# Another search for the selection threshold: six counts placed by secants instead of eight by halving

## The chip, the cores and the metric

The kernel runs on one core of a Trainium2 chip. The metric is the device time of one execution in microseconds (us); the value quoted is the median of several executions of the same program on the same core.

## What is computed

The reference is two transformer-like blocks of a sequence of 2048 rows of width 1024, one after the other. Only the attention of the second block matters here. For each query row it scores all earlier keys with an indexer of eight small heads, keeps the 256 keys with the highest scores, and attends to these alone:

```python
TOPK_MAX = 256
...
logits = jnp.einsum('bqhd,bsd->bqhs', qib.astype(jnp.float32), kf_idx) * (IDX_DIM ** -0.5)
score = jnp.einsum('bqhs,bqh->bqs', jax.nn.relu(logits),
                   wb.astype(jnp.float32)) * (N_IDX_HEADS ** -0.5)
causal = key_pos[None, :] <= q_pos[:, None]
score = jnp.where(causal[None], score, -jnp.inf)
_, sel = lax.top_k(score, k_top)
...
s = jnp.einsum('bqhgd,bqkhd->bqhgk', qg, k_sel.astype(jnp.float32)) * (HEAD_DIM ** -0.5)
s = jnp.where(valid[:, :, None, None, :], s, -jnp.inf)
p = jax.nn.softmax(s, axis=-1)
o = jnp.einsum('bqhgk,bqkhd->bqhgd', p, v_sel.astype(jnp.float32))
```

Here `k_top` is 256, and `k_sel`, `v_sel` are the keys and values picked by `sel`.

## The kernel before

The program is a chain of phases: a convolution mixer, projections, a first attention, projections and rotation of the second block, then `phase_select_attend` (L2359 to L3197), which is the phase of this change, and `phase_out_2`, the last projection. In the trace `phase_select_attend` runs from about 2300 us to 3013 us.

It works on 16 blocks of 128 queries. They are taken in the order `ORDER` (L1927): 0, 1, 4, 6, 8, 10, 12, 14, 15, 13, 11, 9, 7, 5, 3, 2. Block b (its place in that order) has `keys(b)` = 128 × (ORDER[b] + 1) keys, so that the blocks grow from 128 keys to 2048 (b = 8) and shrink again to 384 (b = 15). Keys come in groups of 512 (`GROUP`): blocks 0, 1, 14 and 15 have one group, 2, 3, 12 and 13 two, 4, 5, 10 and 11 three, 6 to 9 four. A block is worked off in four pairs of heads, and a pair in as many steps as it has groups. All engines run through the same written-out list of steps (`units`), each with its own instructions and with semaphores between them. `in_quarter(u, pair, quarter)` picks the step in which a piece of side work is done: quarter q of a pair with G groups is the step q·G//4. With four groups the four quarters are four steps; with three groups quarters 0 and 1 are the same step; with two groups 0 and 1 are one and 2 and 3 the other; with one group all four are one step.

In a step the PE makes score products into five PSUM buffers (L3152, L3153): attention products of a block 1.6 pairs ahead, and indexer products of a block three blocks ahead. VectorE masks the attention products and keeps the row extreme (`mask`, L2918), ScalarE takes the exponential (`raise_e`, L2766), the PE transposes it (L3174), ScalarE copies it out (L2783), and the PE multiplies it with the values (L3188). ScalarE rectifies the indexer products (L2775) and VectorE adds them, weighted, to the score rows of 128 × keys(b) (`add_score`, L2896 and L2899).

14 blocks (2 to 15) have more than 256 keys and need a selection. While block b is attended to, the selection of block b + 1 (`now`) is finished and the threshold of block b + 2 (`soon`) is searched.

The search of `soon` before the change:

- ScalarE sums a sample of the scores (L2796) and the squares (L2803). The Pool makes the mean, a first guess from the normal distribution, and eight halving step widths from the deviation (`start_search`, L2678 to L2690).
- Eight counts follow, each a pass over the whole score row of 128 × keys: four on ScalarE (`count_signs`, L2823: the sum of the signs of guess minus score), in pair 1, quarters 0 and 2, and pair 2, quarters 0 and 2; four on VectorE (`count_at`, L2935: the number of scores at or above the guess), in pair 3, quarters 0 to 3.
- After each count but the last the guess goes up or down by one width. For a count of ScalarE the step is made in two instructions by ScalarE itself (L2827, L2829) in the five blocks 2, 3, 4, 5 and 15 (`local`), and by the Pool (`move_on`, L2697, L2698) in the nine blocks 6 to 14 (`pooled`). For a count of VectorE it is made in two instructions by VectorE (L2938, L2940).

Then the Pool turns the eight counts into missing keys (`sum_up`, L2664 to L2666), and VectorE takes the lowest guess with fewer than 256 keys at or above it, the edge, and the number of keys missing there (`find_edge`, L2948, L2952). Up to 16 missing keys are found by two rounds of the eight largest scores below the edge (L2969, L2977). `set_bias` (L2984, VectorE, pair 1, quarter 3) writes the mask of the block, `keep_causal` (L2727, Pool) its causal part, and the semaphore `biased` lets VectorE go on in `check_selection` (pair 2, quarter 1, at the start of the step), which also reads one number from the Pool (`find_rank`). If some row of the block has no guess with 1 to 16 missing keys, `check_selection` runs `search` and `break_ties` (L2986 to L3028) on VectorE: 31 rounds of a count and three small instructions, one after another. 

The Pool's program is one list: for each block `sum_up` and `rank_wanted` of `now`, `find_mean` and `start_search` of `soon`, `find_rank` of `now`, then the moves of `soon`, with `keep_causal(now)` ahead of the third move (k == 2).

Of the kernel before, what the change touches and what calls it, by code (L numbers as in the profile page):

```python
# [9 lines left out]
ALU = mybir.AluOpType  # L10
# [2348 lines left out]
def phase_select_attend(nc, sem, p_t, rot_hi, rot_lo, bit_int, bit_val, half_powers, rank_row, inverse_t, mix_t, ident, space, w_out):  # L2359
# [14 lines left out]
    COUNTS = 8  # L2374
    ON_ACT = COUNTS // 2
    OVER = 2.0 * SEQ
    EIGHT = 8
    SAMPLE = 4
# [125 lines left out]
    with ExitStack() as ctx:  # L2504
# [30 lines left out]
        halves = al.sb("sa_halves", [P, COUNTS])  # L2535
        width = al.sb("sa_width", [P, 2, COUNTS])
        guess = al.sb("sa_guess", [P, 2, COUNTS])
        go_d = al.sb("sa_go_d", [P, 1])
        go_a = al.sb("sa_go_a", [P, 1])
        go_p = al.sb("sa_go_p", [P, 1])  # L2540
        signs = al.sb("sa_signs", [P, 2, ON_ACT])
        count = al.sb("sa_count", [P, 2, COUNTS - ON_ACT])
        even = al.sb("sa_even", [P, TILES])
# [24 lines left out]
        counted, moved, signed, turned_up = sem("sa_counted"), sem("sa_moved"), sem("sa_signed"), sem("sa_turned_up")  # L2568
# [69 lines left out]
        def _(pool):  # L2638
# [8 lines left out]
            for qb in selecting:  # L2647
                nc.gpsimd.memset(even[:, qb:qb + 1], float(keys(qb) - 2 * TOP) + 0.5).then_inc(consts_set, 1)
# [6 lines left out]
            pool.wait_ge(bits_in, 64)  # L2655
# [22 lines left out]
            def start_search(b):  # L2678
# [8 lines left out]
                then(nc.gpsimd.tensor_scalar(width[:, j], halves[:], sd[:, 0:1], (4.0 if keys(b) < 2 * TOP - P // 2 else 1.25) * SMALL, ALU.mult, ALU.mult))  # L2687
# [760 lines left out]
```

## Time and profile before

| what | us |
|---|---|
| median of 3 runs | 3189.06 |
| lowest and highest run | 3187.68, 3195.86 |
| span of the profiled execution | 3189.0 |
| of it PE busy | 2990.2 (94%) |
| VectorE (DVE) busy | 2253.7 (71%) |
| ScalarE (ACT) busy | 1624.1 (51%) |
| Pool busy | 231.3 (7%) |

The page gives the profiled execution its span, from the first instruction to the last, and no second time; it lies 0.06 us under the median of the runs. "Busy" is the time in which an engine executes instructions; waits for semaphores are not in it. The shares are means over phases of different kinds, so the rows further down are those of the selection phase.

### The profile page before, as it was taken

The page shows a single profiled execution, that of the slowest core. Times are in us where ns is not written, and L with a number is a line of the kernel's source. Part 1 is how long each engine was busy: PE and PEld are TensorE (multiplying, and loading weights), DVE is VectorE, ACT ScalarE, POOL GpSimd, SP SyncE. Part 2 cuts the span into 40 slices and gives each one's busy share as a digit, 9 for nine tenths or more (in the row PEclk, how much of TensorE's full clock was granted, in tenths as well). Part 3 has the DMA queues.
Part 4 walks back from the last instruction along what each step waited for, and adds up shares of the span by engine and source line. Part 5 has one row for each costly group of instructions (what it writes and reads, how often), then busy time and mean ns, then how long its engine had stood idle before and what let it go on. Part 6 is the DMA issues. An engine that isn't in the chain of part 4 may idle for free. (4 is left out here: it accounts for less than half of the span.)

```text
span 3189.0 us, 48176 instructions
## 1 busy us (share of the span) xinstructions
PE 2990.2 (94%) x17460; PEld 2369.3 (74%) x17460; DVE 2253.7 (71%) x3296; ACT 1624.1 (51%) x2947; POOL 231.3 (7%) x519
## 2 busy tenths in 40 slices
PE   6999999999998999999999999999977889998899
PEld 5888788888777866677777777887756666776687
DVE  8888877753677758888878554524378989988543
ACT  5344422232545436777769423211288887887500
POOL 0000000000000001110100000000021321213100
PEclk8999999999999999999999999999989999999899
DMA  4434422244657432111136334232641111011665
GB/s 119 121 109 122 145 67 75 84 141 144 170 171 254 154 131 77 32 37 41 45 92 199 112 96 132 86 132 74 172 98 34 31 28 24 23 36 39 170 183 158
DMA packets 377860, 331.47 MB, mean 104 GB/s; under 512 B 100988, under 2 KB 331900, under 8 KB 371472
## 3 DMA queue, kind: packets, MB, share of 16 engines
q1 hardware_dynamic: 371784, 293.40, 32.4%
q0 software_dynamic: 5120, 34.67, 2.8%
q8 instruction: 142, 2.33, 0.3%
q14 instruction: 94, 0.77, 0.1%
q10 hardware_dynamic: 720, 0.31, 0.1%
HBM read 211.26 MB, written 107.10 MB: 100 GB/s over the span
## 5 line engine op out<-in xcount | busy, mean ns | idle before, releaser
L629 PE MATMUL p_oa_acc<-s_h_a_hi,s_mx_w_hi 128*128 128x512 f32 x768 | 301.8, 393 | 15.2 <-DVE s_h_a_lo L418 9.4
L323 ACT ACTIVATE s_mx_w_hi<-s_mx_raw 128x512 fp32r<-128x512 f32 x224 | 139.1, 629 | 320.6 <-PE p_oa_acc L629 256.8
L629 PE MATMUL p_oa_acc<-s_h_a_lo,s_mx_w_hi 128*128 128x512 f32 x768 | 300.4, 391 | 0.0
L629 PE MATMUL p_oa_acc<-s_h_a_hi,s_mx_w_lo 128*128 128x512 f32 x768 | 300.2, 391 | 0.0
L1598 DVE TENSOR_TENSOR_SCAN s_st_prod<-s_st_soft,s_st_prod 128x512 f32<-128x512 f32 x192 | 234.4, 1267 | 15.9 <-ACT s_st_soft L1525 15.9
L3174 PE MATMUL p_sa_turn<-s_ident,s_sa_arg 128*128 128x128 f32 x1088 | 166.3, 289 | 48.5 <-ACT s_sa_prob L2783 30.9
L1525 ACT ACTIVATE s_st_soft<-p_st_z 128x512 f32<-128x512 f32 (+3 forms) x320 | 153.7, 534 | 112.0 <-PE p_st_z L1650 112.0
L2345 PE MATMUL p_pr_ps<-s_h_hi,s_pr_w_hi 128*128 128x512 f32 (+1 forms) x712 | 195.4, 395 | 1.8 <-PEq L1712 1.2
L2766 ACT ACTIVATE s_sa_arg<-s_sa_arg,s_sa_low_top 128x128 f32<-128x128 f32 (+15 forms) x128 | 155.7, 1218 | 79.6 <-DVE s_sa_low_top L2918 79.6
L460 DVE TENSOR_TENSOR s_mx_w_lo<-s_mx_raw,s_mx_w_hi 128x512 fp32r<-128x512 f32 x224 | 153.5, 685 | 57.8 <-ACT s_mx_w_hi L323 56.3
L2345 PE MATMUL p_pr_ps<-s_h_lo,s_pr_w_hi 128*128 128x512 f32 (+1 forms) x712 | 191.5, 389 | 0.0
L2345 PE MATMUL p_pr_ps<-s_h_hi,s_pr_w_lo 128*128 128x512 f32 (+1 forms) x712 | 191.5, 389 | 0.0
L3174 PEld LDWEIGHTS p_sa_turn<-s_ident,s_sa_arg 128*128 128x128 f32 x1088 | 120.9, 145 | 86.4 <-issue 53.3
L2227 DVE TENSOR_TENSOR s_pr_w_lo<-s_pr_raw,s_pr_w_hi 128x1024 fp32r<-128x1024 f32 (+1 forms) x22 | 26.5, 1204 | 223.5 <-ACT s_pr_w_hi L2168 223.5
L629 PEld LDWEIGHTS p_oa_acc<-s_h_a_hi,s_mx_w_hi 128*128 128x128 f32 x768 | 145.0, 189 | 47.9 <-issue 17.9
L2775 ACT ACTIVATE s_sa_relu<-p_sa_pr 128x512 f32<-128x512 f32 (+3 forms) x304 | 155.5, 567 | 28.0 <-DVE s_sa_score L2899 13.8
L629 PEld LDWEIGHTS p_oa_acc<-s_h_a_hi,s_mx_w_lo 128*128 128x128 f32 x768 | 145.1, 189 | 30.4
L3188 PE MATMUL p_sa_o_sum<-s_sa_prob,s_sa_v_nat 128*64 128x128 f32 x2176 | 160.7, 288 | 7.4 <-ACT s_sa_o L2789 7.4
L629 PEld LDWEIGHTS p_oa_acc<-s_h_a_lo,s_mx_w_hi 128*128 128x128 f32 x768 | 145.2, 189 | 29.6
L2899 DVE SCALAR_TENSOR_TENSOR s_sa_score<-s_sa_relu,s_sa_w_idx,s_sa_score 128x1024 f32<-128x1024 f32 (+7 forms) x154 | 153.8, 1021 | 18.9 <-ACT s_sa_relu L2775 17.9
L3188 PEld LDWEIGHTS p_sa_o_sum<-s_sa_prob,s_sa_v_nat 128*64 128x64 f32 x2176 | 121.2, 141 | 58.9 <-issue 46.3
L2783 ACT ACTIVATE s_sa_prob<-p_sa_turn 128x512 f32<-128x512 f32 (+3 forms) x320 | 154.3, 541 | 11.2 <-PE p_sa_turn L3174 10.7
(379 smaller groups left out, 7408.7 us busy)
## 6 DMA issues: line engine op xcount, KB each, us to landing
s_mx_raw<-in_w_in_a SPq DMA_DIRECT2D x128, 256.0 KB, 3.8
s_pb_ada<-in_w_ada SPq DMA_DIRECT2D x16, 768.0 KB, 4.3
s_pr_raw<-in_w_in SPq DMA_DIRECT2D x21, 512.0 KB, 3.9
s_pr_work<-s_pr_stage SPq DMA_DIRECT2D x38, 256.0 KB, 4.2
d_rot_hi<-s_pr_rot POOLq DMA_DIRECT2D x9, 1024.0 KB, 4.3
d_rot_lo<-s_pr_stage POOLq DMA_DIRECT2D x9, 1024.0 KB, 6.2
d_y_t<-s_mx_y SPq DMA_DIRECT2D x16, 512.0 KB, 5.5
s_oa_y_raw<-d_y_t SPq DMA_DIRECT2D x16, 512.0 KB, 4.8
```

What stands on the lines that cost most here:

```text
L323: nc.scalar.activation(w_hi[:, m], raw[g % 2][:, m], ACT.Copy).then_inc(hi_done, 1)
L460: nc.vector.tensor_tensor(w_lo[:, m], raw[g % 2][:, m], w_hi[:, m].bitcast(F32), ALU.subtract).then_inc(lo_done, 1)
L629: ins = nc.tensor.matmul(bank, w[:, m, k, :], a[:, m, k, :], start=(k == 0 and n == 0), stop=(k == KH - 1 and n == 2))
L1525: nc.scalar.activation(soft[:, u % DEEP, s, 0:n], z[u % 2 * 2 + s][:, 0:n], ACT.Sigmoid, scale=-SCALE).then_inc(softened, 1)
L1598: nc.vector.tensor_tensor_scan(prod[:, b, s, 0:n][:, ::-1], back, back, carry, ALU.mult, ALU.bypass).then_inc(multiplied, 1)
L2345: ins = nc.tensor.matmul(ps[b % 2][0:cols, t * 512:(t + 1) * 512], w[b % 2][:, k, 0:cols], a[:, k, t * 512:(t + 1) * 512], start=(k == 0 a ...
L2766: nc.scalar.activation(row, row, ACT.Exp, scale=-1.0, bias=low_top[:, s % DEEP, side, len(parts(qb)) - 1:len(parts(qb))], accum_out=total[ ...
L2775: nc.scalar.activation(relu[:, a % R_DEEP, half:half + n], pr[p % BANKS][:, 0:n], ACT.Relu).then_inc(relu_done, 1)
L2783: nc.scalar.activation(prob[:, u % P_DEEP, side, 0:w], turn[turn_of["prob", u, side] % 2][:, 0:w], ACT.Copy).then_inc(p_ready, 1)
L2899: ins = nc.vector.scalar_tensor_tensor(s, relu[:, a % R_DEEP, 0:n], w, s, ALU.mult, ALU.add)
L3174: ins = nc.tensor.transpose(turn[i % 2][:, c:c + P], arg[:, s % DEEP, side, at + c:at + c + P], ident[:])
L3188: ins = nc.tensor.matmul(o_ps[side * HD:side * HD + HD, pair * P:pair * P + P], v_nat[:, (at + c) // P, kv * HD:kv * HD + HD], prob[:, u % ...
```

## The change

The number of counts goes from eight to six: three on ScalarE (pair 1, quarters 0 and 2; pair 2, quarter 0) and three on VectorE (pair 2, quarter 2; pair 3, quarters 0 and 2). All five moves between them are made by the Pool, in all 14 blocks, and their size comes from the number of keys missed: the first by the slope of the normal distribution, the next two by a secant through the last two counts, with its slope held between a quarter and four times the normal one, the last two by the last slope, damped by 0.7 and 0.5. The aim is 248 keys (256 − 8). A secant needs one over the square of the rise; VectorE makes it (`flatten`, one RECIPROCAL of 128 × 1) between two instructions of the Pool, in pair 1, quarter 3, and pair 2, quarter 1. The Pool's `keep_causal(now)` stays ahead of the third move, and so behind the first secant. `find_edge` waits for all five moves instead of for VectorE's own steps. The constants for the halving (one small DMA, 14 memsets) go away.

```diff
-    COUNTS = 8
-    ON_ACT = COUNTS // 2
+    COUNTS = 6
+    ON_ACT = 3
+    STEEP, FLAT = 0.25, 4.0
+    SECANTS, DAMPED = 2, {3: 0.7, 4: 0.5}
-    pooled = [b for b in selecting if b - 2 in blocks and keys(b - 2) >= WIDE]
-    local = [b for b in selecting if b not in pooled]
+    MOVES = COUNTS - 1
+    def aim(qb):
+        return float(keys(qb) - 2 * (TOP - EIGHT))
+    def first_slope(qb):
+        at = start_point(qb)
+        return math.sqrt(2.0 * math.pi) * math.exp(at * at / 2.0) / (2.0 * (keys(qb) - P // 2))
...
-                then(nc.gpsimd.tensor_scalar(width[:, j], halves[:], sd[:, 0:1], (4.0 if keys(b) < 2 * TOP - P // 2 else 1.25) * SMALL, ALU.mult, ALU.mult))
+                for n, share in enumerate((1.0, STEEP, FLAT)):
+                    then(nc.gpsimd.tensor_scalar(slopes[:, j, n:n + 1], sd[:], first_slope(b) * share * SMALL, None, ALU.mult))
...
             def move_on(b, k):
-                at, step, half = guess[:, j, k:k + 1], width[:, j, k:k + 1], width[:, j, k + 1:k + 2]
-                pool.wait_ge(signed, ON_ACT * i + k + 1)
-                then(nc.gpsimd.tensor_scalar(go_p[:], signs[:, j, k:k + 1], float(keys(b) - 2 * TOP) + 0.5, step, ALU.is_lt, ALU.mult))
-                nc.gpsimd.tensor_scalar(guess[:, j, k + 1:k + 2], go_p[:], half, at, ALU.subtract, ALU.add).then_inc(moved_on, 1)
+                at, here, to = guess[:, j, k:k + 1], level[:, j, k:k + 1], guess[:, j, k + 1:k + 2]
+                if k < ON_ACT:
+                    pool.wait_ge(signed, ON_ACT * i + k + 1)
+                    then(nc.gpsimd.tensor_scalar(here, signs[:, j, k:k + 1], -aim(b), None, ALU.add))
+                else:
+                    pool.wait_ge(counted, (COUNTS - ON_ACT) * i + k - ON_ACT + 1)
+                    then(nc.gpsimd.tensor_scalar(here, count[:, j, k - ON_ACT:k - ON_ACT + 1], -2.0, keys(b) - aim(b), ALU.mult, ALU.add))
+                if k == 0:
+                    then(nc.gpsimd.tensor_scalar(move[:], here, slopes[:, j, 0:1], None, ALU.mult))
+                elif k <= SECANTS:
+                    then(nc.gpsimd.tensor_scalar(rise[:], here, level[:, j, k - 1:k], None, ALU.subtract))
+                    nc.gpsimd.tensor_scalar(square_rise[:], rise[:], rise[:, 0:1], 1.0, ALU.mult, ALU.max).then_inc(risen, 1)
+                    then(nc.gpsimd.tensor_scalar(run[:], at, guess[:, j, k - 1:k], rise[:, 0:1], ALU.subtract, ALU.mult))
+                    pool.wait_ge(flattened, SECANTS * i + k)
+                    then(nc.gpsimd.tensor_scalar(slope[:], run[:], per_rise[:, 0:1], slopes[:, j, 1:2], ALU.mult, ALU.max))
+                    then(nc.gpsimd.tensor_scalar(slope[:], slope[:], slopes[:, j, 2:3], None, ALU.min))
+                    then(nc.gpsimd.tensor_scalar(move[:], here, slope[:, 0:1], None, ALU.mult))
+                else:
+                    then(nc.gpsimd.tensor_scalar(move[:], here, slope[:, 0:1], DAMPED[k], ALU.mult, ALU.mult))
+                nc.gpsimd.tensor_scalar(to, move[:], -1.0, at, ALU.mult, ALU.add).then_inc(moved_on, 1)
...
-                for k in range(ON_ACT):
+                for k in range(MOVES):
                     if k == 2 and now in selecting:
                         keep_causal(now)
-                    if soon in pooled:
+                    if soon in selecting:
                         move_on(soon, k)
...
             def count_signs(b, k):
-                if k and b in pooled:
-                    act.wait_ge(moved_on, ON_ACT * pooled_to(b) + k)
-                elif k:
-                    act.wait_ge(turned_up, done)
+                if k:
+                    act.wait_ge(moved_on, MOVES * i + k)
...
-                if b in pooled:
-                    return
-                act.wait_ge(signed, ON_ACT * i + k + 1)
-                nc.scalar.activation(go_a[:], c, ACT.Sign, scale=-1.0, bias=even[:, b:b + 1]).then_inc(turned_up, 1)
-                act.wait_ge(turned_up, done + 1)
-                nc.scalar.activation(guess[:, j, k + 1:k + 2], go_a[:], ACT.Identity, scale=width[:, j, k + 1:k + 2], bias=at).then_inc(turned_up, 1)
...
-                for k, (pair, quarter) in enumerate(((1, 0), (1, 2), (2, 0), (2, 2))):
+                for k, (pair, quarter) in enumerate(((1, 0), (1, 2), (2, 0))):
                     if in_quarter(u, pair, quarter) and soon:
                         count_signs(soon, k)
...
+            def flatten(b, k):
+                dve.wait_ge(risen, SECANTS * place_of(b) + k)
+                nc.vector.reciprocal(per_rise[:], square_rise[:]).then_inc(flattened, 1)
+
             def count_at(b, k):
+                dve.wait_ge(moved_on, MOVES * i + k)
...
-                if k + 1 < COUNTS:
-                    dve.wait_ge(counted, steps * i + c + 1)
-                    nc.vector.tensor_scalar(go_d[:], total_k, float(TOP), width[:, j, k:k + 1], ALU.is_ge, ALU.mult).then_inc(moved, 1)
-                    dve.wait_ge(moved, done + 1)
-                    nc.vector.tensor_scalar(guess[:, j, k + 1:k + 2], go_d[:], width[:, j, k + 1:k + 2], at, ALU.subtract, ALU.add).then_inc(moved, 1)
...
                 if in_quarter(u, 1, 3) and now:
                     set_bias(now)
-                for k, (pair, quarter) in enumerate(((3, 0), (3, 1), (3, 2), (3, 3))):
+                for k, (pair, quarter) in enumerate(((1, 3), (2, 1))):
+                    if in_quarter(u, pair, quarter) and soon:
+                        flatten(soon, 1 + k)
+                for k, (pair, quarter) in enumerate(((2, 2), (3, 0), (3, 2))):
                     if in_quarter(u, pair, quarter) and soon:
                         count_at(soon, ON_ACT + k)
```

## Rows read from the trace of the kernel before

**Rows 1.** The page's first line.
```profile
span 3189.0 us, 48176 instructions
```

**Rows 2.** Stretches, one per block (1, 4, 6, 8), and the sum of all 16.
```profile
2345.00:2379.00 34.00, 23.61 (x121) 18.00 (x122) 27.20 (x66) 26.72 (x69) 9.94 (x23) 0.85 0.28 55
...
2472.00:2528.00 56.00, 47.58 (x336) 36.22 (x334) 51.84 (x95) 46.84 (x91) 15.37 (x31) 0.97 0.14 29
...
2586.00:2651.00 65.00, 55.64 (x436) 41.62 (x435) 60.20 (x112) 52.97 (x95) 14.07 (x30) 1.00 0.12 26
...
2713.00:2773.00 60.00, 57.41 (x500) 45.18 (x499) 54.76 (x111) 51.38 (x89) 13.20 (x31) 1.00 0.12 28
...
sum 690.00, PE 594.59 PEld 460.05 DVE 585.06 ACT 559.53 POOL 163.38; mean PE 37.16 PEld 28.75 DVE 36.57 ACT 34.97 POOL 10.21
```

The columns of rows 2 are: stretch, its length, then busy us (and instructions) of PE, PE weight load, DVE, ACT, POOL, then TensorE's granted clock, the DMA share and GB/s.

**Rows 3.** Waits of DVE, then of PE, 2310 to 3010 us: total, times, longest.
```profile
DVE s_sa_arg L2918 <- PE p_sa_pr L3153: 49.7, 57, 3.6
DVE s_sa_score L2899 <- ACT s_sa_relu L2775: 16.5, 12, 2.4
...
PE p_sa_pr L3152 <- DVE s_sa_low_top L2918: 30.9, 24, 4.2
```

**Rows 4.** Groups by line on DVE, 2310 to 3010 us: busy, mean ns, idle before.
```profile
L2935 DVE TENSOR_SCALAR_CACHE_REDUCE s_sa_junk_d<-s_sa_score,s_sa_guess 128x640 bf16<-128x640 f32 (+13 forms) x56 | 82.7, 1477 | 0.8
...
L2940 DVE TENSOR_SCALAR s_sa_guess<-s_sa_go_d,s_sa_width,s_sa_guess 128x1 f32<-128x1 f32 x42 | 11.5, 273 | 1.5
...
L2938 DVE TENSOR_SCALAR s_sa_go_d<-s_sa_count,s_sa_width 128x1 f32<-128x1 f32 x42 | 9.0, 214 | 1.5
...
L2935 DVE DVE_READ_ACCUMULATOR s_sa_junk_d<-s_sa_score,s_sa_guess 128x1 f32 x56 | 4.7, 83 | 0.0
L3045 DVE RECIPROCAL s_sa_inverse<-s_sa_total 128x8 f32<-128x8 f32 x16 | 3.2, 198 | 1.2 <-ACT s_sa_arg L2766 1.2
```

**Rows 5.** Groups by line on ACT, 2310 to 3010 us.
```profile
L2823 ACT ACTIVATE s_sa_junk_a<-s_sa_score,s_sa_guess 128x640 bf16<-128x640 f32 (+13 forms) x56 | 74.2, 1324 | 0.3 <-POOL s_sa_guess L2698 0.2
...
L2823 ACT ACTIVATION_READ_ACCUMULATOR s_sa_junk_a<-s_sa_score,s_sa_guess 128x1 f32 x56 | 12.0, 214 | 0.0
...
L2829 ACT ACTIVATE s_sa_guess<-s_sa_go_a,s_sa_guess,s_sa_width 128x1 f32<-128x1 f32 x20 | 7.7, 387 | 0.7
L2827 ACT ACTIVATE s_sa_go_a<-s_sa_signs,s_sa_even 128x1 f32<-128x1 f32 x20 | 5.9, 295 | 0.6
```

**Rows 6.** Groups by line on POOL, 2310 to 3010 us.
```profile
L2698 POOL TENSOR_SCALAR s_sa_guess<-s_sa_go_p,s_sa_width,s_sa_guess 128x1 f32<-128x1 f32 x36 | 14.2, 393 | 3.8
L2697 POOL TENSOR_SCALAR s_sa_go_p<-s_sa_signs,s_sa_width 128x1 f32<-128x1 f32 x36 | 14.0, 388 | 132.6 <-ACT s_sa_junk_a L2823 132.6
```

**Rows 7.** Instructions of L2727: shortest, median and longest in ns, first and last start.
```profile
L2727 POOL TENSOR_SCALAR_AFFINE_SELECT s_sa_bias<-s_sa_bias x14: 294/1196/1199, 2355.2 to 2973.8; 128x128 bf16<-128x128 bf16 x14
```

**Rows 8.** In order of time, block 2 (two groups): start us, length us.
```profile
2394.12 0.63 DVE L2984 TENSOR_SCALAR s_sa_bias<-s_sa_place 128x896 bf16<-128x896 f32 x1
...
2395.39 0.19 ACT L2823 ACTIVATION_READ_ACCUMULATOR s_sa_junk_a<-s_sa_score,s_sa_guess 128x1 f32 x1
...
2398.28 0.08 DVE L2918 DVE_READ_ACCUMULATOR2_ANT s_sa_low_top<- 128x1 f32 x1
...
2400.48 0.22 ACT L2823 ACTIVATION_READ_ACCUMULATOR s_sa_junk_a<-s_sa_score,s_sa_guess 128x1 f32 x1
```

**Rows 9.** The same of block 4 (three groups); in brackets idle time before and releaser.
```profile
2499.81 0.19 ACT L2823 ACTIVATION_READ_ACCUMULATOR s_sa_junk_a<-s_sa_score,s_sa_guess 128x1 f32 x1
...
2501.37 1.15 DVE L2899 SCALAR_TENSOR_TENSOR s_sa_score<-s_sa_relu,s_sa_w_idx,s_sa_score 128x896 f32<-128x896 f32 x1 [1.72 <-ACT s_sa_relu L2775]
```

**Rows 10.** The same of block 6 (four groups).
```profile
2614.66 0.22 ACT L2823 ACTIVATION_READ_ACCUMULATOR s_sa_junk_a<-s_sa_score,s_sa_guess 128x1 f32 x1
...
2616.39 1.16 DVE L2984 TENSOR_SCALAR s_sa_bias<-s_sa_place 128x1920 bf16<-128x1920 f32 x1
```

More of the change, by code:

```diff
@@ L2534, in phase_select_attend @@
         sd = al.sb("sa_sd", [P, 1])
-        halves = al.sb("sa_halves", [P, COUNTS])
-        width = al.sb("sa_width", [P, 2, COUNTS])
+        slopes = al.sb("sa_slopes", [P, 2, 3])
         guess = al.sb("sa_guess", [P, 2, COUNTS])
-        go_d = al.sb("sa_go_d", [P, 1])
-        go_a = al.sb("sa_go_a", [P, 1])
-        go_p = al.sb("sa_go_p", [P, 1])
+        level = al.sb("sa_level", [P, 2, COUNTS])
+        rise = al.sb("sa_rise", [P, 1])
+        square_rise = al.sb("sa_square_rise", [P, 1])
+        per_rise = al.sb("sa_per_rise", [P, 1])
+        run = al.sb("sa_run", [P, 1])
+        slope = al.sb("sa_slope", [P, 1])
+        move = al.sb("sa_move", [P, 1])
         signs = al.sb("sa_signs", [P, 2, ON_ACT])
         count = al.sb("sa_count", [P, 2, COUNTS - ON_ACT])
-        even = al.sb("sa_even", [P, TILES])
         lack = al.sb("sa_lack", [P, COUNTS])
@@ L2646, in _ @@
             nc.gpsimd.memset(tiny_var[:], 1e-12).then_inc(consts_set, 1)
-            for qb in selecting:
-                nc.gpsimd.memset(even[:, qb:qb + 1], float(keys(qb) - 2 * TOP) + 0.5).then_inc(consts_set, 1)
             for qb in blocks:
@@ L2841, in _ @@
             act.dma_start(v_raw[:, 0], p_t[ROW_V:ROW_V + P, 0:GROUP]).then_inc(v_in[0], 16)
-            for to, rows in ((halves, half_powers), (ranks, rank_row), (bit_i, bit_int), (bit_f, bit_val)):
+            for to, rows in ((ranks, rank_row), (bit_i, bit_int), (bit_f, bit_val)):
                 act.dma_start(to[:], rows.partition_broadcast(P)).then_inc(bits_in, 16)
@@ L2911, in mask @@
                     else:
-                        dve.wait_ge(consts_set, 2 + len(selecting) + qb)
+                        dve.wait_ge(consts_set, 2 + qb)
                 dve.wait_ge(product, p + 1)
@@ L2919, in mask @@
                                                scalar=before, op0=ALU.add, op1=ALU.min, accum_out=low_top[:, s % DEEP, side, m:m + 1]).then_inc(masked, 1)
+            def flatten(b, k):
+                dve.wait_ge(risen, SECANTS * place_of(b) + k)
+                nc.vector.reciprocal(per_rise[:], square_rise[:]).then_inc(flattened, 1)
             def count_at(b, k):
                 n, i, j, c = keys(b), place_of(b), b % 2, k - ON_ACT
[L2924 to L2932 removed]
+                dve.wait_ge(moved_on, MOVES * i + k)
                 if c == 0 and i >= 2:
                     dve.wait_ge(lacking, i - 1)
[L2935 to L2940 removed]
+                nc.vector.tensor_scalar(junk_d[:, 0:n], score[:, b % AHEAD, 0:n], guess[:, j, k:k + 1], None, ALU.is_ge, ALU.add,
+                                        accum_out=count[:, j, c:c + 1]).then_inc(counted, 1)
             def find_edge(b):
@@ L2944, in find_edge @@
                 dve.wait_ge(lacking, i + 1)
-                dve.wait_ge(moved, 2 * (COUNTS - ON_ACT - 1) * (i + 1))
+                dve.wait_ge(moved_on, MOVES * (i + 1))
                 if i:
@@ L3413, in program @@
             space.before_selection(Alloc(nc, third))
-            phase_select_attend(nc, between, p_t, rot_hi, rot_lo, a["bit_int"], a["bit_val"], a["half_powers"], a["rank_row"], inverse_t, mix_t, ident,
+            phase_select_attend(nc, between, p_t, rot_hi, rot_lo, a["bit_int"], a["bit_val"], a["rank_row"], inverse_t, mix_t, ident,
                                 space, a["w_out_2"][0])
```

28 lines of the change are left out of this document (7 added, 21 removed).

## The prediction

> **What bounds the kernel now.** The sum goes by the profiled execution, whose span [rows 1] is the median of the runs to 0.1 us. I read first the busy time of the stretches between blocks, because the change touches one phase of about 700 us. Over its 16 blocks no engine is full: of 690 us PE is busy 595, DVE 585, ACT 560, the Pool 163 [rows 2]. It differs by block. In block 1 none reaches 81%; in blocks 4 and 6 DVE leads with 93%, PE has 85%; in block 8 PE leads with 96%, DVE has 91% [rows 2]. So DVE or ACT time taken away is worth most in the small blocks and the rise, and little in the middle. Next the waits: DVE stands 49.7 us waiting for score products and 16.5 us for rectified scores, and PE stands 30.9 us because DVE has not emptied a product buffer [rows 3]. DVE and PE wait for each other in turns, so a DVE delay can be made up only partly, and a DVE saving is passed on only partly. Then the groups by line give the prices, and the order of time gives the places where the new waits fall.
>
> **What goes.** On DVE, one count in four: (82.7 + 4.7)/4 = 21.9 us; 42 steps, 11.5 + 9.0 = 20.5 us; and the gaps ahead of these, about 3 us [rows 4]. That is 45.4 us. On ACT, one count in four, (74.2 + 12.0)/4 = 21.6 us, and the 20 own steps, 7.7 + 5.9 = 13.6 us: 35 us [rows 5]. The removed DMA and memsets lie ahead of the first block, while the engines wait for other loads: nothing.
>
> **What comes.** DVE gets 28 reciprocals of 128x1. The nearest row is one of 128x8 at 198 ns [rows 4]: 5.5 us at most, and I take that. DVE is 40 us lighter. Spread over blocks (the count by its keys, the rest evenly, 1.3 us each): 13.7 us in the four-group blocks 6 to 9, 12.0 in the three-group ones (4, 5, 10, 11), 14.1 in the six of one or two groups (0 to 3, 12, 13).
>
> The Pool gets 25 instructions of one column a block for its moves (3 + 8 + 8 + 3 + 3) and two more slopes: 14 × 27 = 378 for 72. One costs 0.39 us and a gap of 3.8/36 = 0.11: 0.5 us [rows 6]. That is some 150 us more, and 163 + 150 still is under half of 690: the Pool does not become the bound by its sum. Its replies matter.
>
> **New waits.** A secant is a round trip: ACT counts, the Pool makes three instructions (1.5 us), DVE the reciprocal, the Pool four more (2.0 us). DVE waits in its fixed order, and behind it wait the adds and masks that empty the product buffers, so PE too.
>
> (a) First reciprocal, behind `set_bias`. In block 2 ACT's second count is read out at 2395.6; plus 1.5 is 2397.1. DVE ends `set_bias` at 2394.75 [rows 8]: it stands 2.3 us. This is the pattern of the five blocks with one or two groups that have both selections (1, 2, 3, 12, 13), where count and reciprocal fall in one step or nearly: 11.5 us. In block 6 the count ends at 2614.9, the square is there at 2616.4, and `set_bias` runs until 2617.55 [rows 10]: nothing, and so in the blocks of three and four groups.
>
> (b) Second reciprocal. In block 2 it comes behind a mask that ends at 2398.4, and ACT's third count ends at 2400.7, so the square at 2402.2 [rows 8]: 3.8 us. The later two-group blocks have shorter counts; I take 2.5 for each of the four. Blocks 0 and 1, where the next count also sits in the same step and needs the four last Pool instructions: 2 us each. Together 14 us. With three groups, the square in block 4 would be there at 2501.5, and DVE already stood idle until 2501.37, for ACT [rows 9]: nothing. With four groups the count is a step ahead: nothing.
>
> (c) `biased`. `keep_causal` is now behind the first secant. After the reciprocal it is 2.0 us of moves and up to 1.2 us of its own [rows 7], 3.2 us; DVE has two adds or so before `check_selection` (about 1.9 us). In the nine blocks with fewer than four groups the check is in the very next step: 1.3 us each, 11.7 us. With four groups a step lies between.
>
> Together 37 us of DVE standing, as against 40 us of DVE work. That is why this is no simple gain.
>
> **The sum.** Savings: in the four-group blocks PE is as full as DVE, so half, 6.9 us; with three groups two thirds, 8.0; in the small blocks all, 14.1; 29 us. ACT's 35 us: 16.5 us of DVE's idle time are for ACT's relu [rows 3], part of it behind a count, as in block 4 [rows 9]; one of four counts goes: 3 us. Together 32 us. Waits: DVE stands now for PE 49.7 us in 57 places [rows 3], and a stand of 2 us just ahead of one of these is free; I let a third of the 37 us vanish so: 25 us stay. Net 7 us: **3189 − 7 = 3182 us**. A measurement of this kernel can tell about 0.3%, 9.6 us, from no change, so the likeliest reading is "within". The bounds: all of 40 us and no wait, 3149; half of the DVE saving and all waits, 3206.
>
> **Where row and rule meet.** The same `keep_causal` of 128x128 takes 294 ns at its shortest and 1196 ns in the median [rows 7], so a Pool instruction can be stretched fourfold by what runs beside it. The mean of 0.39 us for a one-column step holds such stretches at the rate they had. The Trainium skill (GPSIMD Engine Reference, Specifications) says that the Pool shares its SBUF interfaces with VectorE and is in contention with DVE instructions that have two SBUF inputs. The rows agree. That rule speaks against moving steps to the Pool; what it gives is the third rival. It holds least where it would hurt most: while DVE stands in (a) or (b) it runs nothing that could be in the way.
>
> **Rivals.**
> 1. *The waits are hidden* (0.22). The stands fall where DVE would have waited for PE; for: 49.7 us of such idle time. Savings of three quarters, 30 us, plus 3 of ACT, minus 6: 3162 us.
> 2. *The waits stay, the other side* (0.17). A stand of DVE in pair 1, quarter 3, or pair 2, quarter 1, fills the five product buffers, PE stops, and ACT's exponentials come later, so that the next count comes later as well. For: PE already stands 30.9 us for a mask [rows 3]. Savings at half, 20 us, waits whole, 37: 3206 us. It decides from the point where DVE stands longer than PE needs to fill the five buffers.
> 3. *The Pool is stretched* (0.04). Each of its chain's seven instructions takes 1.2 instead of 0.5 us: (a) and (b) 2.1 us longer at 11 places, (c) 2.8 at nine: 48 us, two thirds on the path: 3214 us.
> 4. *The search misses* (0.05). One row without a guess that misses 1 to 16 keys sets off 31 rounds on DVE, each a mean count of 1.56 us and three small steps of 0.25 [rows 4]: 72 us a block. 3182 + 72 = 3254 us. Against it: with 384 keys, of which the first row of the block sees 257, and normal scores, the guesses find by my working 199, 230 and 242 keys, inside the window of 240 to 255 at the third of six counts; bigger blocks start closer. But eight halvings cannot run away, and secants on a skewed row can.
>
> **Chances.** The forecast holds 0.52: 0.13 of it below 3179.5, 0.38 within 9.6 us of no change, 0.01 above. Rival 1 is faster (0.22); rival 2 slower by 0.15 and within by 0.02; rivals 3 and 4 slower (0.09). So faster 0.35, within 0.40, slower 0.25. The range goes from 3165, short of rival 1, to 3206, rival 2: below it lies 0.10, above it rivals 3 and 4. The forecast's own range is 3173 to 3192.
>
> **What would show it.** DVE busy in the phase falls by 40 us, ACT by 35, the Pool rises by 150. The waits list shows the reciprocal on DVE waiting for the Pool, some 25 us in 11 to 14 places, all in blocks of one or two groups, and DVE waiting for `biased` after it. Blocks 6 to 9 get shorter by about 1.7 us each, blocks 1 to 3, 12 and 13 stay or grow. I am wrong if the reciprocal's waits are under 10 us or over 45, if blocks of four groups show them, if the Pool's mean is above 0.6 us, or if rows of `search` appear.

## The result and the profile after

| | before | after |
|---|---|---|
| median of the runs, us | 3189.06 (3187.68 to 3195.86, 5 runs) | 3204.92 (3197.91 to 3208.25, 5 runs) |
| span of the profiled execution, us | 3189.0 | 3202.9 |

The ratio is 1.0041, with a 95% interval of 1.0027 to 1.0056: the changed kernel is 0.4% slower, 13 us (the two medians lie 16 us apart). The time lies inside the range, at its upper end, and on the other side of no change than the forecast. It is almost the time of rival 2 (3206 us).

The page of the changed kernel, its first line and its part 1:

```profile
span 3202.9 us, 48344 instructions
...
PE 3004.3 (94%) x17460; PEld 2384.2 (74%) x17460; DVE 2215.4 (69%) x3212; ACT 1596.7 (50%) x2879; POOL 335.6 (10%) x811
```

DVE is busy 38 us less than before, ACT 27 less, the Pool 104 more. PE is busy 14 us more. The selection phase grew from 713 us (2300 to 3013) to 727:

```profile
2300.00:3027.00 727.00, 623.50 (x4610) 487.44 (x4611) 558.22 (x1168) 548.55 (x1079) 270.81 (x697) 0.91 0.23 51
```

So the work went as intended and the time did not. The same blocks as in [rows 2], 1, 4, 6 and 8, same columns, in the changed kernel:

```profile
2348.00:2388.00 40.00, 27.02 (x122) 20.75 (x121) 24.76 (x60) 23.26 (x59) 18.22 (x50) 0.70 0.25 49
2485.00:2543.00 58.00, 50.15 (x336) 38.39 (x334) 47.93 (x89) 45.59 (x88) 22.63 (x50) 0.91 0.13 29
2602.00:2662.00 60.00, 55.09 (x441) 41.99 (x439) 56.91 (x113) 51.44 (x94) 22.41 (x51) 1.00 0.12 28
2721.00:2778.00 57.00, 56.29 (x498) 44.97 (x496) 52.02 (x111) 49.61 (x86) 18.04 (x51) 1.00 0.13 30
```

Block 1 takes 6 us more and block 4 two, blocks 6 and 8 take 5 and 3 less. I took the length of each block from the starts of ACT's copies of the outputs (15 starts in each trace), and that of block 0 from PE's first instruction of the phase, which starts at 2300.4 us before and in the changed kernel, and at 2304.3 us in the profiled execution of `six_halving`. By the number of groups, in us against before:

| blocks | changed kernel | `six_halving`, below |
|---|---|---|
| four groups (6 to 9) | −13.9 | −14.9 |
| three groups (4, 5, 10, 11) | +4.1 | −7.5 |
| one or two groups (0 to 3, 12 to 14) | +24.0 | −9.0 |

What takes the time back stands in the list of waits of the changed kernel, 2310 to 3030 us (total, times, longest):

```profile
ACT s_sa_arg L2788 <- DVE s_sa_low_top L2931: 92.8, 63, 7.1
...
DVE s_sa_per_rise L2937 <- POOL s_sa_square_rise L2712: 54.7, 19, 7.6
...
DVE s_sa_arg L2931 <- PE p_sa_pr L3162: 42.0, 54, 3.0
...
PE p_sa_pr L3161 <- DVE s_sa_low_top L2931: 36.3, 22, 5.2
...
DVE s_sa_arg L2931 <- issue: 20.0, 8, 3.4
...
DVE s_sa_junk_d L2945 <- POOL s_sa_guess L2720: 9.3, 11, 1.8
```

Against [rows 3]: the wait for products fell from 49.7 to 42.0 us and PE's wait for a mask rose from 30.9 to 36.3. New are 54.7 us ahead of the reciprocals and 9.3 us ahead of DVE's counts for a guess of the Pool. "issue" in front of a mask is the stand ahead of `check_selection`, which waits for `biased` and reads a number before it; it was 4.9 us in 5 places before. DVE's wait for ACT's relu, 16.5 us before, is 1.5 us.

The "issue" row holds only a part of the stands for `biased`. In block 4 the same stand is named after a product:

```profile
2510.95 0.29 POOL L2749 TENSOR_SCALAR_AFFINE_SELECT s_sa_bias<-s_sa_bias 128x128 bf16<-128x128 bf16 x1
...
2512.28 0.75 DVE L2931 CUSTOM_DVE_ANT_0 s_sa_arg<-p_sa_pr,s_sa_bias,s_sa_low_top 128x512 f32<-128x512 f32 x1 [2.60 <-PE p_sa_pr L3162]
```

The mask comes 1.04 us after the end of `keep_causal`. Read in order of time, a mask starts 1.03 to 1.71 us after that end, with idle time of over 0.15 us before it, in all 14 blocks that have a selection to finish, under either name. I call this idle time the mask stand. It sums to 31.3 us in the changed kernel and to 10.8 us (9 blocks) in the kernel before.

The moved work in order of time, block 2 (start, length; in brackets idle time before and who ended it):

```profile
2404.71 0.19 ACT L2842 ACTIVATION_READ_ACCUMULATOR s_sa_junk_a<-s_sa_score,s_sa_guess 128x1 f32 x1
...
2405.01 0.39 PE L3161 MATMUL p_sa_pr<-s_sa_ki_qi_q 128*128 128x512 f32 x1
...
2405.68 0.30 POOL L2712 TENSOR_SCALAR s_sa_square_rise<-s_sa_rise 128x1 f32<-128x1 f32 x1
...
2406.02 0.16 DVE L2937 RECIPROCAL s_sa_per_rise<-s_sa_square_rise 128x1 f32<-128x1 f32 x1 [2.29 <-POOL s_sa_square_rise L2712]
2406.10 1.82 DVE L2912 SCALAR_TENSOR_TENSOR s_sa_score<-s_sa_relu,s_sa_w_idx,s_sa_score 128x1024 f32<-128x1024 f32 x2
...
2406.44 1.56 POOL L2715 TENSOR_SCALAR s_sa_slope<-s_sa_run,s_sa_per_rise,s_sa_slopes 128x1 f32<-128x1 f32 x1
...
2408.10 0.29 POOL L2716 TENSOR_SCALAR s_sa_slope<-s_sa_slope,s_sa_slopes 128x1 f32<-128x1 f32 x1
...
2409.09 0.29 POOL L2749 TENSOR_SCALAR_AFFINE_SELECT s_sa_bias<-s_sa_bias 128x128 bf16<-128x128 bf16 x1
2410.77 0.69 DVE L2931 CUSTOM_DVE_ANT_0 s_sa_arg<-p_sa_pr,s_sa_bias 128x512 f32<-128x512 f32 x1 [2.85 <-issue]
...
2411.61 0.77 PE L3161 MATMUL p_sa_pr<-s_sa_k_hi,s_sa_ki_qi_q 128*128 128x512 f32 x1 [4.20 <-DVE s_sa_low_top L2931]
```

These 7 us show the first reciprocal and the mask stand. ACT's count ends at 2404.90. Three Pool instructions later DVE, which stood 2.29 us, makes the reciprocal and two adds; the Pool makes four more instructions of its chain and `keep_causal`, which ends at 2409.38. The first mask of the next step comes only at 2410.77. Then PE, which stood 4.20 us with its buffers full, takes 0.77 us for a product that took 0.39 us before the stand.

Block 4 has three groups, and its second reciprocal:

```profile
2513.46 0.09 DVE L2931 DVE_READ_ACCUMULATOR2_ANT s_sa_low_top<- 128x1 f32 x1
...
2513.58 1.26 ACT L2788 ACTIVATE s_sa_arg<-s_sa_arg,s_sa_low_top 128x1152 f32<-128x1152 f32 x1 [3.48 <-DVE s_sa_low_top L2931]
...
2514.84 1.67 ACT L2842 ACTIVATE s_sa_junk_a<-s_sa_score,s_sa_guess 128x1664 bf16<-128x1664 f32 x1
2516.41 0.19 ACT L2842 ACTIVATION_READ_ACCUMULATOR s_sa_junk_a<-s_sa_score,s_sa_guess 128x1 f32 x1
...
2517.71 0.16 DVE L2937 RECIPROCAL s_sa_per_rise<-s_sa_square_rise 128x1 f32<-128x1 f32 x1 [4.16 <-POOL s_sa_square_rise L2712]
```

DVE's last mask of the step releases ACT's exponential; ACT counts behind it, the Pool makes three instructions, and the reciprocal, next on DVE, has stood 4.16 us. In the kernel before DVE spent this same stretch on the adds and masks of the next step:

```profile
2496.86 0.08 DVE L2918 DVE_READ_ACCUMULATOR2_ANT s_sa_low_top<- 128x1 f32 x1
2496.86 1.28 DVE L2899 SCALAR_TENSOR_TENSOR s_sa_score<-s_sa_relu,s_sa_w_idx,s_sa_score 128x1024 f32<-128x1024 f32 x1
...
2498.06 0.68 DVE L2918 CUSTOM_DVE_ANT_0 s_sa_arg<-p_sa_pr,s_sa_bias 128x512 f32<-128x512 f32 x1
...
2498.89 0.75 DVE L2918 CUSTOM_DVE_ANT_0 s_sa_arg<-p_sa_pr,s_sa_bias,s_sa_low_top 128x512 f32<-128x512 f32 x1
```

### The profile page after: what moved, and what is told of

Read it like the earlier page. It is cut to its first block and busy times, and to the rows that moved or that the text cites. A ratio compares the mean times of both kernels' runs of the same rounds, so it can differ in the third digit from the quotient of the medians.

```text
span 3202.9 us, 48344 instructions
## 1 busy us (share of the span) xinstructions
PE 3004.3 (94%) x17460; PEld 2384.2 (74%) x17460; DVE 2215.4 (69%) x3212; ACT 1596.7 (50%) x2879; POOL 335.6 (10%) x811
## 5 line engine op out<-in xcount | busy, mean ns | idle before, releaser
L1598 DVE TENSOR_TENSOR_SCAN s_st_prod<-s_st_soft,s_st_prod 128x512 f32<-128x512 f32 x192 | 234.4, 1268 | 17.6 <-ACT s_st_soft L1525 17.6
L2345 PEld LDWEIGHTS p_pr_ps<-s_h_hi,s_pr_w_hi 128*128 128x128 f32 (+1 forms) x712 | 132.1, 186 | 35.7 <-issue 5.9
```

The lines of the kernel that those rows point to most:

```text
L1598: nc.vector.tensor_tensor_scan(prod[:, b, s, 0:n][:, ::-1], back, back, carry, ALU.mult, ALU.bypass).then_inc(multiplied, 1)
L2345: ins = nc.tensor.matmul(ps[b % 2][0:cols, t * 512:(t + 1) * 512], w[b % 2][:, k, 0:cols], a[:, k, t * 512:(t + 1) * 512], start=(k == 0 a ...
```

## The experiments

My theory: two counts fewer are worth some 32 us, and the stands of DVE behind the Pool's replies take them back, each nearly whole. Rivals: the Pool's added work slows everything beside it (rival 3), or the saving was never there. Each ratio is against the kernel before on the same chip, in the same rounds; its medians were 3191.79 us (experiments 1 and 2), 3192.7 us (`mask_late`, `after_causal`, `six_pool_load`, `late_spread`) and 3194.07 us (`six_pool_after`, `six_causal`). Where two variants are compared, their ratios are.

**1. The two counts alone: `six_halving`.** The kernel before, with six halvings instead of eight, in the positions of the changed kernel, and each engine making its own steps as before. The last line of the edit leaves the repair search out; no row of it appears in the kernel before either, so it takes no time in both.

```diff
-    COUNTS = 8
+    COUNTS = 6
...
-                for k, (pair, quarter) in enumerate(((1, 0), (1, 2), (2, 0), (2, 2))):
+                for k, (pair, quarter) in enumerate(((1, 0), (1, 2), (2, 0))):
...
-                for k, (pair, quarter) in enumerate(((3, 0), (3, 1), (3, 2), (3, 3))):
+                for k, (pair, quarter) in enumerate(((2, 2), (3, 0), (3, 2))):
...
-                then(nc.gpsimd.tensor_scalar(report[:], found[:, 0:1], 0.5, huge[:, b % 2:b % 2 + 1], ALU.is_lt, ALU.add))
+                then(nc.gpsimd.tensor_scalar(report[:], found[:, 0:1], -1.0, huge[:, b % 2:b % 2 + 1], ALU.is_lt, ALU.add))
```

> The kernel before, with six halving counts instead of eight (three of ScalarE, three of VectorE, in the steps of the changed kernel), and each engine still making its own steps. The repair search is switched off, since some rows may miss. It shows what two counts fewer are worth without any answer from the Pool. Theory (the counts are worth their price and the changed kernel loses it in VectorE's waits): DVE busy falls by 14 counts and 28 of its own steps' instructions, some 36 us, ACT by 22 to 25, and the time by 20 to 30 us, to 3159 to 3169. Rival A (neither engine is on the path, so the counts are worth little): 3180 to 3189. Rival B (the counts moved to earlier steps do the harm): slower than 3189.

Measured: 3159.91 us (3156.47 to 3162.7, 4 runs) against 3191.79, ratio 0.9898 [0.9883, 0.9913]: 32 us less. The saving is there, for less work taken away than expected: DVE is busy 28 us less (36 expected), ACT 20 (22 to 25). DVE stands here for guesses too, with no secant in the program, since its first count now lies in pair 2, quarter 2; the kernel before has no such row:

```profile
DVE s_sa_junk_d L2935 <- POOL s_sa_guess L2698: 8.4, 5, 2.3
DVE s_sa_junk_d L2935 <- ACT s_sa_guess L2829: 7.8, 3, 3.7
```

**2. The waits one by one.** Three kernels take them away in turn. `one_secant` makes only the first secant and keeps its slope:

```diff
-    SECANTS, DAMPED = 2, {3: 0.7, 4: 0.5}
+    SECANTS, DAMPED = 1, {2: 1.0, 3: 0.7, 4: 0.5}
...
-                for k, (pair, quarter) in enumerate(((1, 3), (2, 1))):
+                for k, (pair, quarter) in enumerate(((1, 3),)):
```

> The changed kernel with one secant instead of two: the third move takes the slope of the second, and the second reciprocal (pair 2, quarter 1) is gone. Theory (VectorE's stand for the reciprocal is the loss; the second one stands 34 of 54.7 us): DVE's wait for the Pool falls from 54.7 to about 20 us and the time by 15 to 25 us, to 3180 to 3190. Rival A (the Pool's many instructions beside VectorE are the loss): only 70 of 378 Pool instructions of the moves go, so 3 us or less, 3202. Rival B (the check behind keep_causal is the loss): no change.

`late_secant` makes the same secant, but takes its reciprocal a place later, in pair 2, quarter 1, and makes the second move with 0.8 of the normal slope meanwhile:

```diff
-    SECANTS, DAMPED = 2, {3: 0.7, 4: 0.5}
+    SECANTS, DAMPED = 1, {2: 1.2, 3: 0.8, 4: 0.6}
...
-                for k, (pair, quarter) in enumerate(((1, 3), (2, 1))):
+                for k, (pair, quarter) in enumerate(((2, 1),)):
...
-                    pool.wait_ge(flattened, SECANTS * i + k)
...
+                    then(nc.gpsimd.tensor_scalar(move[:], here, slopes[:, j, 0:1], 0.8, ALU.mult, ALU.mult))
+                else:
+                    if k == 2:
+                        pool.wait_ge(flattened, i + 1)
```

> The changed kernel with the one secant used a move later: the second move takes 0.8 of the normal slope, the rise of the first two counts is inverted by VectorE in pair 2, quarter 1, a step or more after it is known, and used from the third move on. The Pool's instructions are as many as in the run with one secant, less none. Theory: no reciprocal is waited for outside block 0, DVE's wait for it falls under 5 us, keep_causal comes 1.5 to 2 us earlier, and the time falls by 25 to 40 us, to 3165 to 3180, under the kernel before. Rival A (the Pool's load): as with one secant, 3200. Rival C (each stand is only passed on to the next wait, for PE's products): DVE's waits for score products grow by what the reciprocal's fall, and the time stays over 3195.

`late_causal` is `late_secant` with `keep_causal` one place earlier in the Pool's list, ahead of the second move:

```diff
-                    if k == 2 and now in selecting:
+                    if k == 1 and now in selecting:
                         keep_causal(now)
```

> The run with the late secant, with keep_causal(now) ahead of the second move instead of the third. Theory: the wait for the mask in pair 2, quarter 1 (20 us in the changed kernel, 5 in the one before) goes back to about 5, and the time falls by another 3 to 8 us against the late secant. Rival (this wait is hidden by others, or is moved to ScalarE's third count, which now waits for set_bias through the Pool): within 2 us of the late secant.

| kernel | median (lowest to highest, runs), us | ratio [95%] | DVE waits for: reciprocal, guess, "issue", us | mask stand, us |
|---|---|---|---|---|
| changed | 3204.92 (3197.91 to 3208.25, 5) | 1.0041 [1.0027, 1.0056] | 54.7, 9.3, 20.0 | 31.3 |
| `one_secant` | 3191.92 (3185.74 to 3197.38, 11) | 0.9996 [0.9987, 1.0006] | 19.2, 19.1, 17.7 | 31.8 |
| `late_secant` | 3179.26 (3175.09 to 3182.31, 5) | 0.9957 [0.9944, 0.9971] | 0, 27.6, 27.0 | 30.5 |
| `late_causal` | 3166.94 (3165.48 to 3170.5, 5) | 0.9923 [0.991, 0.9937] | 0, 27.8, 10.1 | 12.6 |

By the ratios, of 3189 us, the second reciprocal cost 0.45%, 14 us, the first 0.39%, 12 us, and the mask behind the Pool's moves 0.34%, 11 us. `one_secant` ended 2 us above the 3180 to 3190 us expected. `late_secant` lies in its range, but its `keep_causal` did not help: the mask stand is 30.5 us, hardly less than in `one_secant`. `late_causal` gained more than the 3 to 8 us expected. Not all of a stand comes back: with the second reciprocal 35.5 us of reciprocal waits go, while the waits for guesses grow by 9.8 us and those for products by 16.4. The waits of `one_secant` and of `late_causal`, 2310 to 3030 us:

```profile
DVE s_sa_arg L2931 <- PE p_sa_pr L3162: 58.4, 65, 3.0
...
DVE s_sa_per_rise L2937 <- POOL s_sa_square_rise L2712: 19.2, 6, 6.2
DVE s_sa_junk_d L2945 <- POOL s_sa_guess L2720: 19.1, 11, 3.4
DVE s_sa_arg L2931 <- issue: 17.7, 8, 3.4
```

```profile
DVE s_sa_arg L2932 <- PE p_sa_pr L3163: 39.8, 58, 1.7
...
DVE s_sa_junk_d L2946 <- POOL s_sa_guess L2721: 27.8, 14, 4.3
...
DVE s_sa_arg L2932 <- issue: 10.1, 6, 2.4
```

**3. The mask alone, in both kernels.** `mask_late` is the kernel before with five one-column Pool instructions, some 2 us, between the wait for `set_bias` and `keep_causal`; `after_causal` is the changed kernel with `keep_causal` one place earlier.

```diff
                 pool.wait_ge(bias_set, place_of(b) + 1)
+                idle_steps(5)
```

> The kernel before, with five one-column Pool instructions (2 to 2.5 us) between the wait for set_bias and keep_causal in every block, and nothing else: the late mask alone, without counts, reciprocals or moves changed. Theory (a mask released 2 to 3 us later makes VectorE stand in pair 2, quarter 1, in the blocks with fewer than four groups): the idle time ahead of the first mask rises from 4.9 to 15 to 25 us and the time by 5 to 12 us, to 3196 to 3203. Rival (it is hidden by VectorE's adds): within 3 us of the kernel before.

> The changed kernel with keep_causal(now) ahead of the second move (the first secant) instead of behind it; both reciprocals stay. Theory: the idle time ahead of the first mask falls from 20 to about 5 to 10 us, but in the blocks of three and four groups, where the square was ready when set_bias ended, the first secant now starts only after set_bias, so that the first reciprocal stands there 1.5 to 2 us, 12 to 16 us in eight blocks: the time is 3195 to 3206, little gained. Rival (only the late mask counts): 3190 or less.

| kernel | median (lowest to highest, runs), us | ratio [95%] |
|---|---|---|
| `mask_late` | 3210.05 (3204.7 to 3218.9, 5) | 1.0049 [1.0035, 1.0063] |
| `after_causal` | 3196.64 (3188.3 to 3200.5, 11) | 1.0008 [0.9999, 1.0017] |

2 us in front of the mask cost the kernel before 16 us (0.49%), more than I had expected, none of it in blocks 6 to 9 (65.1, 62.1, 59.7 and 54.9 us, as before) and about 2 us in nearly every other block. The "issue" waits rise only from 4.9 to 12.3 us, but the mask stand rises from 10.8 to 31.7 us, in 13 blocks: the phase is longer by about what DVE stands longer (19 us in the profiled executions, from PE's first instruction of the phase to its last). PE's wait for a mask in `mask_late` (2340 to 3033 us), 30.9 us before:

```profile
PE p_sa_pr L3159 <- DVE s_sa_low_top L2925: 42.3, 28, 4.2
```

In the changed kernel the earlier `keep_causal` gives 11 us back and lies in the range expected. The mask stand falls from 31.3 to 1.5 us, and 14 us of it come back ahead of the reciprocals: 68.8 us instead of 54.7. The first of DVE's waits in `after_causal`:

```profile
DVE s_sa_per_rise L2937 <- POOL s_sa_square_rise L2712: 68.8, 28, 7.6
```

**4. The Pool's load without its replies.** `six_pool_load` is `six_halving` with 294 further one-column Pool instructions, seven behind each turn of the moves.

```diff
                     if soon in pooled:
                         move_on(soon, k)
+                    if soon in selecting:
+                        idle_steps(7)
```

> The run of six halving counts with 21 more one-column Pool instructions in each of the 14 searches (294 in all, about as many as the change adds), after the moves, on a tile that nobody else reads. It prices the Pool's load by itself. Theory (the waits were the loss, not the load): within 4 us of the six halving counts, 3160 to 3164. Rival A (instructions of the Pool beside VectorE cost VectorE time): 10 us or more above them, 3170 and up, and the mean of VectorE's adds and masks grows by 1% or more.

Measured: 3182.79 us (3181.99 to 3187.42, 7 runs) against 3192.7, ratio 0.9971 [0.996, 0.9982]: 23 us more than `six_halving`. That looked like rival 3. But two of the three sevens of each block stand ahead of `keep_causal` (k = 0 and 1), and DVE's "issue" waits are 17.6 us, against 5.6, its mask stand 31.7 us, against 11.8. DVE's adds did not grow by the 1% that rival A of the expectation names: 1019 ns in the mean of 154, against 1020. So the same 294 instructions were put where nothing waits behind them, and beside it `keep_causal` was moved forward in `six_halving`:

```diff
                     if soon in pooled:
                         move_on(soon, k)
+                if soon in selecting:
+                    idle_steps(21)
```

> As six_halving (six halving counts, the repair search left out), with 21 one-column instructions on the Pool in each of the 14 selecting blocks, 294 in all, as many as in six_pool_load, but all behind the last move of the block's turn, so that they stand ahead of nothing that DVE or ACT waits for in that block, and ahead of keep_causal in no turn. Own theory (the Pool's work itself costs nothing, only what is queued behind it): 3156 to 3166 us, six_halving's 3160, with DVE's waits of issue under 9 us. Rival (the Pool's work stretches the work of the others, wherever it stands): 3175 to 3185 us, as six_pool_load.

> As six_halving, with keep_causal one place earlier in the Pool's queue (at k == 1), ahead of the second move. Own theory (the late mask costs only because the secant's wait stands ahead of it; two halving instructions do not delay it beyond DVE's first need): 3153 to 3161 us, DVE's waits of issue from 5.6 to 2 to 6 us. Rival (an earlier mask is worth 12 us in any kernel, as late_causal against late_secant): 3144 to 3150 us.

| kernel | median (lowest to highest, runs), us | ratio [95%] |
|---|---|---|
| `six_pool_after` | 3162.61 (3161.07 to 3169.05, 5) | 0.991 [0.9894, 0.9926] |
| `six_causal` | 3164.28 (3157.51 to 3167.45, 5) | 0.9905 [0.9888, 0.9921] |

The Pool's group of added instructions, in `six_pool_load` and then in `six_pool_after` (busy us, mean ns, idle before), and DVE's "issue" waits of each:

```profile
L2652 POOL TENSOR_SCALAR s_sa_idle<-s_sa_idle 128x1 f32<-128x1 f32 x294 | 87.7, 298 | 21.6
...
DVE s_sa_arg L2926 <- issue: 17.6, 5, 6.2
```

```profile
L2652 POOL TENSOR_SCALAR s_sa_idle<-s_sa_idle 128x1 f32<-128x1 f32 x294 | 81.4, 277 | 23.2
...
DVE s_sa_arg L2926 <- issue: 5.6, 5, 1.8
```

The same load costs 23 us in one place and nothing that can be told in the other (0.991 against 0.9898, the intervals overlap). The Pool's sum of work is not the cause; what is queued behind it is. `six_causal` ended 3 us above the range I had given it, and its mask stand is 10.4 us: an earlier `keep_causal` is worth nothing that can be told where no long chain stands in front of it.

**5. A version faster than the kernel before.** `late_causal` still stands 27.8 us for guesses of the Pool. `late_spread` puts DVE's three counts later and lets `keep_causal` stay behind the second move in blocks of four groups.

```diff
-                    if k == 1 and now in selecting:
+                    if k == (1 if len(parts(qb)) < 4 else 2) and now in selecting:
...
-enumerate(((2, 2), (3, 0), (3, 2))):
+enumerate(((3, 0), (3, 2), (3, 3))):
```

> The run with the late secant, with keep_causal ahead of the second move only in blocks of fewer than four groups, and VectorE's three counts in pair 3, quarters 0, 2 and 3, instead of pair 2, quarter 2, and pair 3, quarters 0 and 2. In the run before this one VectorE stood 27.8 us for guesses, 25 of it ahead of its first count, and ScalarE 8 us in the four-group blocks behind keep_causal. Theory: the first count's stands go, one answer of about 1 us stays in the small blocks, VectorE's wait for guesses falls under 12 us and the time to 3150 to 3162, under the six halving counts. Rival (a stand taken away only comes back as a wait for score products, or the last count, now later, holds up find_edge): 3164 to 3170.

Measured: 3158.72 us (3153.09 to 3161.39, 4 runs) against 3192.7, ratio 0.989 [0.9875, 0.9905], 35 us less than before, with the repair search in place and no row of it in the trace. Its waits for guesses are 6.5 us, its mask stand is 12.2 us. From `six_halving` (0.9898) it can't be told apart.

## Why the prediction was wrong, point by point

- **What goes and comes.** DVE −40 us predicted, −38 measured; ACT −35 and −27; the Pool +150 and +104, of which the prediction's 150 counted the gaps too. A reciprocal takes 163 ns in the median, 4.6 us for 28, as against 5.5.
- **What the savings are worth.** 32 us predicted, 32 measured (`six_halving`), but by errors that cancel. The prediction let 40 us less of DVE work pass on as 29 us; `six_halving` has 28 us less of it, since DVE still makes its own steps there, and the time falls by 32. By blocks the predicted DVE part was 6.9, 8.0 and 14.1 us; the trace of `six_halving` gives 14.9, 7.5 and 9.0, with DVE's busy time down by 11.6, 6.6 and 10.4. In the four-group blocks the saving passes on whole, although PE is as full there. The predicted 1.7 us for each of blocks 6 to 9 was 5.4, 3.2, 2.6 and 2.7.
- **(a) First reciprocal.** 11.5 us predicted. In block 2, from whose rows it was worked out, the stand is 2.29 us as against 2.3. In the five blocks named it is 12.7 us in all (2.73, 2.29, 1.59, 2.76, 3.34). What was missing is block 0, 7.59 us: all its pair is one step, and the "two groups" pattern was not carried to it. In all 20.3 us. The blocks of three and four groups show none, as predicted.
- **(b) Second reciprocal: the step that failed.** 14 us predicted, 34.4 measured. The prediction put nothing for three groups, because "DVE already stood idle until 2501.37". The rows of block 4 show what was overlooked. The reciprocal stands in DVE's program behind the last mask of its own step, which ended at 2496.94 in the kernel before, and not at the later idle point: between the two DVE did an add and two masks of the next step, which now wait behind the reciprocal. The right sum was mask to exponential to count to three Pool instructions: 1.26 + 1.67 + 0.19 + 1.1 us, 4.2 us. Blocks 4, 5, 10 and 11 stand 4.16, 4.59, 3.95 and 3.52 us: 16.2 us, more than the net of 7 us on which the forecast rested. With four groups the prediction held (0.9 us in four blocks).
- **(c) `biased`.** 11.7 us predicted. The mask stand rose by 20.5 us (31.3 against 10.8), of which the "issue" row shows 15.1. In the nine blocks named it is 1.8 us each instead of 1.3; the four-group blocks, for which nothing was predicted, add 4.3. From reciprocal to the end of `keep_causal` it is 3.36 us in block 2, against 3.2 predicted. But DVE's first mask comes 1.39 us after that, and between the two lie the number that `check_selection` reads and its branch, for which the prediction has no term.
- **(d), not in the prediction.** Guesses of the Pool that come late for DVE's counts, 9.3 us. They are no loss against `six_halving`, which stands 16.2 us there: they come of the earlier places of DVE's counts, and its 32 us contain them.
- **The share that vanishes.** A third of 37 us was to vanish. Against `six_halving`, DVE stands 54.7 us more for reciprocals and 19.5 us more for the mask (31.3 against 11.8), and 6.9 us less for guesses: 67 us. The time is 45 us longer (3204.92 − 3159.91, and the same by the ratios). So two thirds stay, and up to four fifths if the changed kernel's 10 us less of DVE work (2215.4 against 2225.4) counts as a saving lost as well. The share was about right; the term it was taken of was half of what was measured: 37 us against 75 (20.3 + 34.4 + 20.5).
- **Rival 2** had the mechanism (PE's wait for a mask is 36.3 us, against 30.9 before and 14.0 in `six_halving`) and the time, 3206 us, but that by two errors that cancel: 20 us of savings where 32 were measured, 37 us for the waits where it was 45.
- **The other rivals.** Rival 1 (waits hidden) falls with experiments 1 and 2. Rival 3: a Pool instruction is stretched, by the rows of block 2: the slope takes 1.56 us beside DVE's adds, the next one 0.29. The Trainium skill (GPSIMD Engine Reference, Specifications) names DVE instructions with two SBUF inputs as those that the Pool is in contention with, and the adds have two: the trace agrees. But the mean of the 350 instructions of the moves is 0.41 us, under the bound of 0.6, and `six_pool_after` shows that the load by itself costs nothing that can be told. One part of rival 3 stays open: the stretched slope stands between the reciprocal and `keep_causal`, so it is a part of (c), and no run takes it away alone. Rival 4: no rows of `search` appear.
- **The chances.** One sign of the list of what would prove me wrong came true, reciprocal waits over 45 us; the three-group blocks, where 16.2 us of them lie, were not in the list. With these blocks in the sum, 37 would have been 53 us, two thirds of it 35 us, and the forecast 3192 us: this step alone turns the sign. The rest is (a), 8.8 us, most of it block 0, (c), 8.8 us, and the other blocks of (b), 4.2 us. With all three as measured, two thirds of 75 us and the saving of 32 give 3207 us.

## What to carry to other kernels

A wait put into an in-order queue is to be priced from the last instruction ahead of it in program order, not from where the engine next stood idle in the old trace: everything it did in between now comes behind the wait. A shorter computation with replies between engines can lose to a longer one without them; here one secant used a move later, in place of two used at once, gained 27 us (1.0041 against 0.9957), since DVE's reciprocals then wait for nothing. Side work on a near-idle engine is free by its sum, and dear by its place: 2 us ahead of a flag for which DVE, and through it PE and ACT, wait cost 16 us over 14 blocks, and 294 instructions behind it, 81 us of the Pool, nothing that can be told. And a list of waits names one releaser for each stand: the stands for `biased` showed whole only by their distance to the end of `keep_causal`, 1.03 to 1.71 us.

## What I had not expected of the hardware

- More stands of PE go with a lower clock behind them. In block 1 the granted clock fell from 0.85 [rows 2] to 0.70, and the same work went from 23.61 us busy to 27.02; in block 4, for the same 336 matmuls, from 0.97 to 0.91 and from 47.58 to 50.15 us. In block 2 a product of 128x512 took 0.77 us after PE had stood 4.20 us, twice the 0.39 us of before the stand: the lower of its two levels, 1.2 GHz instead of 2.4. Over the phase that is 10.7 us of PE's time for the same 4610 matmuls (612.81 before, 623.50 after), at a granted clock of 0.94 and 0.91. The stretch behind the stand in block 2, same columns as [rows 2]:

```profile
2411.60:2414.00 2.40, 2.39 (x6) 1.92 (x7) 0.36 (x2) 1.99 (x4) 0.00 (x0) 0.50 0.00 0
```

- The stretch between Pool and DVE goes one way. The slope (L2715) takes 1107 ns in the mean of 28, as it starts right when DVE goes on to its adds, and the other one-column steps 233 to 658 ns. In seven of the 28 places no add was under way when it started, and it took 366 to 372 ns; in the other 21 it lasted until 0.08 to 0.25 us after the end of that add, or of the one that followed it at once, up to 2368 ns. DVE's adds take 1022 ns in the mean, as against 1024 before:

```profile
L2715 POOL TENSOR_SCALAR s_sa_slope<-s_sa_run,s_sa_per_rise,s_sa_slopes 128x1 f32<-128x1 f32 x28 | 31.0, 1107 | 12.4 <-DVE s_sa_per_rise L2937 10.2
...
L2720 POOL TENSOR_SCALAR s_sa_guess<-s_sa_move,s_sa_guess 128x1 f32<-128x1 f32 x70 | 19.0, 271 | 7.5
```

```profile
L2912 DVE SCALAR_TENSOR_TENSOR s_sa_score<-s_sa_relu,s_sa_w_idx,s_sa_score 128x1024 f32<-128x1024 f32 (+7 forms) x152 | 151.9, 1022 | 2.2 <-ACT s_sa_relu L2797 1.5
```

- Between the flag and the first mask lie a read of a number and a branch. Where DVE stands there, the mask comes 1.03 to 1.71 us after the end of `keep_causal`, 1.39 us in block 2 of the changed kernel; the kernel before shows the same spread (1.04 to 1.71 us). Where `keep_causal` was done early enough, as in block 6 before (it ends at 2618.63 us, the first mask of the next step starts at 2621.43), DVE shows no idle time there. What of it is the read and what the branch was not tried.
